# One decoder layer on one core: the stage behind the input projection ordered anew, a triple of weight slots between any two groups of small products, and page values and weights interleaved on SyncE

## The reference, cut to what matters

```python
h = rmsnorm(x) * (1 + scale1(c)) + shift1(c)
p = h @ w_in                       # 21 tiles of 128 columns here
#   NSA:   compressed blocks, top-16 selected blocks, window of 512, mixed by gates
#   mLSTM: 4 heads, chunkwise with running max; the samples one step from a state
#   pool:  trailing means over 2/4/8/16, a linear map per group
x = x + gate1(c) * (concat(nsa, mlstm, pool) @ w_out)
h = rmsnorm(x) * (1 + scale2(c)) + shift2(c)
x = x + gate2(c) * ((silu(a) * b) @ w_down)   # [a, b] = conv3(h @ w_up)
```

## Time and profile before

| | us |
|---|---|
| median of three runs | 843.7 (842.22 to 844.24) |
| the profiled execution | 844.35 |
| its span | 842.2 |
| TensorE busy, share of the span | 778.6 (92%) |
| VectorE | 516.3 (61%) |
| ScalarE | 329.5 (39%) |
| GpSimd | 308.1 (37%) |

### The profile page before, as it was taken

How to read it: one execution, slowest core, us unless ns; L and a number is a source line. 1 busy time by engine, 2 the same in 40 slices (tenths; PEclk the granted TensorE clock), 3 DMA queues, 4 the chain that set the end, 5 groups by cost and what they waited for, 6 DMA issues and landing times.

```text
span 842.2 us, 18847 instructions
## 1 busy us (share of the span) xinstructions
PE 778.6 (92%) x7517; PEld 717.9 (85%) x7517; DVE 516.3 (61%) x1026; ACT 329.5 (39%) x601; POOL 308.1 (37%) x163
## 2 busy tenths in 40 slices
PE   2899989999988898999989999999999999999994
PEld 2798979988866566669978999999999999999993
DVE  3745799994676799743765666665222676665324
ACT  4422322333241466643335554552213545544221
POOL 0042657572000344452422443444434434344440
PEclk9999999999698699998999999999999999999997
DMA  9964777786579544423721344342332432322312
GB/s 355 327 227 133 232 234 258 248 270 224 198 278 380 97 120 124 97 74 111 311 76 51 101 126 124 101 124 78 101 100 90 126 119 95 101 89 87 97 49 101
DMA packets 73141, 131.23 MB, mean 156 GB/s; under 512 B 12684, under 2 KB 47388, under 8 KB 72800
## 3 DMA queue, kind: packets, MB, share of 16 engines
q1 hardware_dynamic: 66928, 114.32, 42.3%
q10 hardware_dynamic: 6096, 15.73, 5.3%
q0 software_dynamic: 32, 0.00, 0.0%
HBM read 124.56 MB, written 9.12 MB: 159 GB/s over the span
## 4 chain that ended last, share of the span: by engine, by line
PE 77%; DVE 12%; issue 4%; DMA 3%; ACT 2%; SPq 1%; POOL 0%; DVEq 0%; ACTq 0%; POOLq 0%
PE ps L668 58%; PE ps L1016 2%; PE ps L1001 2%; PE ps L1038 2%; PE ps L1054 2%; PE ps L760 1%; DMA arena<-weights 1%; DMA raw<-weights 1%; DMA arena<-cache_keys 1%; DVE arena L2090 1%; PE ps L919 1%; PE ps L753 1%; DVE sq L1480 1%; PE ps L890 1%; DVE arena L1504 1%
## 5 line engine op out<-in xcount | busy, mean ns | idle before, releaser
L668 PE MATMUL ps<-hR,wR 128*128 128x260 f32 x3456 | 429.3, 286 | 7.8 <-ACT hR L1144 2.7
L668 PEld LDWEIGHTS ps<-hR,wR 128*128 128x128 f32 x3456 | 422.6, 191 | 12.4 <-issue 6.3
L631 POOL TENSOR_TENSOR wR<-raw,wR 128x1024 fp32r<-128x1024 f32 x92 | 225.4, 2450 | 298.7 <-ACT wR L1136 298.7
L1136 ACT ACTIVATE wR<-raw 128x1024 fp32r<-128x1024 f32 x94 | 99.5, 1058 | 214.6 <-PE ps L668 210.0
L668 PE MATMUL ps<-fR,wR 128*128 128x260 f32 x1056 | 128.1, 283 | 2.3 <-DVE fR L2061 2.0
L668 PEld LDWEIGHTS ps<-fR,wR 128*128 128x128 f32 x1056 | 127.0, 188 | 3.1 <-DVE fR L2061 2.4
L2085 DVE COPY arena<-arena 128x2 f32<-128x2 f32 x44 | 47.7, 1084 | 93.5 <-ACT arena L1427 93.5
L624 POOL TENSOR_SCALAR arena<-arena,fac 128x128 f32<-128x128 f32 (+3 forms) x32 | 40.3, 1263 | 133.0 <-DVE fac L1984 133.0
L612 POOL TENSOR_TENSOR arena<-arena,par 128x512 f32<-128x512 f32 x32 | 42.4, 1326 | 79.7 <-DMA arena<-cache_keys 75.1
L2046 DVE TENSOR_TENSOR t<-ps,mod 128x8 f32<-128x8 f32 x24 | 4.0, 167 | 108.7 <-PE ps L668 108.7
L1360 ACT ACTIVATE arena<-ps,nmx 128x128 f32<-128x128 f32 (+3 forms) x64 | 33.1, 524 | 19.8 <-DVE nmx L1975 19.7
(11 more groups left out here) (369 smaller groups left out, 845.3 us busy)
## 6 DMA issues: line engine op xcount, KB each, us to landing
raw<-weights SPq DMA_DIRECT2D x95, 512.0 KB, 3.7
arena<-cache_keys SPq DMA_DIRECT2D x128, 192.0 KB, 3.5
arena<-weights SPq DMA_DIRECT2D x27, 512.0 KB, 10.1
arena<-cache_values SPq DMA_DIRECT2D x128, 64.0 KB, 2.0
raw<-weights ACTq DMA_DIRECT2D x12, 512.0 KB, 8.5
arena<-weights ACTq DMA_DIRECT2D x9, 512.0 KB, 7.9
x<-xT SPq DMA_DIRECT2D x16, 260.0 KB, 4.0
out_y<-x SPq DMA_DIRECT2D x8, 260.0 KB, 2.2
```

The costliest lines, as they stand in the source:

```text
L631: nc.gpsimd.tensor_tensor(w_slot(i)[:, 1, :, :], raw[:, g % RAW, :, :], w_slot(i)[:, 0, :, :].bitcast(F32), ALU.subtract).then_inc(lo_read ...
L668: last = mm(ps[:, a + half, 0:TH], w_slot(i)[:, wp, k, :], src[:, hp, j, half * TH:(half + 1) * TH], start=(j == 0 and q == 0), stop=(j == ...
L1136: A(w_slot(i)[:, 0, :, :], raw[:, g % RAW, :, :], ACT.Identity).then_inc(hi_ready, 1)
```

## The change

On TensorE the helpers are called in another order; ScalarE's and VectorE's lists follow. `sample_rows` is cut into four helpers, and its products for the value rows go with those for the query and key rows (192 columns in one product instead of 128 and 64). The pool products use banks 4, 5 and 7 instead of 0, 1 and 6, and the turns of the mLSTM result banks 0 and 1; `side_mix` goes, and `scores(0)` waits for `mmix_ready`. ScalarE issues no weights in this stage any more; SyncE does, between the pages. `spread` is issued ahead of the window keys, and these in parts of six and two sequences. The window values go ahead of five outputs, and the first three slots of `w_out` behind the pages of sequences 2 and 3.

```diff
 # SyncE
-            sp.wait_ge(comp_done, 2 * NB)
-            sp.wait_ge(slc_scored, 2 * NB)
-            for b in range(0, NB, 4):
-                sp.dma_start(kwin[:, b:b + 4, :], winK[:, b:b + 4, :]).then_inc(win_landed, 16)
+            sp.wait_ge(rows_ready, 1)
+            sp.dma_start(spread, mro[0:4, :]).then_inc(side_landed, 16)
+            for half, first, last in ((2 * NB - 1, 0, 6), (2 * NB, 6, 8)):
+                sp.wait_ge(comp_done, half)
+                sp.wait_ge(slc_scored, half)
+                sp.dma_start(kwin[:, first:last, :], winK[:, first:last, :]).then_inc(win_landed, 16)
...
+            load_rows(2)
+            load_rows(3)
+            for g in range(N_A + RAW + EXTRA, N_A + 5 * RAW):
+                load_slot(g)
...
             sp.wait_ge(wsc_done, 2)
             load_values(0)
-            load_values(1)
+            for g in range(N_A + 5 * RAW, N_A + 7 * RAW):
+                load_slot(g)
+            load_value_half(1, 0)
+            for g in range(N_A + 7 * RAW, len(PART1)):
+                load_slot(g)
+            load_value_half(1, 1)
             sp.dma_start(cst[:, :], mC).then_inc(rec_landed, 16)
             sp.dma_start(o_fm, pT[:, T_KC:T_MK, 0:S]).then_inc(early_out, 16)
             sp.dma_start(o_vn, vn[:, :, :]).then_inc(early_out, 16)
+            sp.wait_ge(slot_done, len(PART1))
+            sp.wait_ge(mmix_ready, 1)
+            load_window(0)
+            load_window(1)
...
             load_values(2)
             load_values(3)
+            for g in range(len(PART1), len(PART1) + RAW):
+                load_slot(g)
 # TensorE: sample_rows cut up, the new order
+            def sample_heads(first):
+                for hh in range(first, first + 2):
+                    sel = every[:, 24 - 8 * hh:24 - 8 * hh + P]
+                    three = sn[0:NB, 0:768].rearrange("p (t h d) -> p t h d", t=3, h=4)[:, :, hh, :]
+                    mm(ps[:, 6, 0:192].rearrange("p (t d) -> p t d", t=3), sel, three, start=(hh == 0), stop=(hh == 3))
...
+            block_sums()
             triple(0)
             compressed_scores()
-            gate_columns()
+            triple(1)
+            sample_rows()
+            sample_heads(0)
             chunk_scores(0)
-            sample_rows()
-            block_sums()
+            window_scores(0)
+            sample_heads(2)
             chunk_scores(1)
+            sample_gates()
+            triple(2)
+            output_gates()
+            window_scores(1)
+            inside(0)
             triple_turn(0)
-            window_scores(0)
-            triple(1)
-            inside(0)
-            window_scores(1)
             chunk_scores(2)
+            inside(1)
+            triple(3)
+            chunk_scores(3)
             triple_turn(1)
             window_rows()
-            inside(1)
-            triple(2)
-            chunk_scores(3)
-            triple_turn(2)
-            triple(3)
             across(0)
             across(1)
+            triple(4)
+            triple_turn(2)
+            triple(5)
             triple_turn(3)
-            triple(4)
             inside(2)
+            triple(6)
             triple_turn(4)
             inside(3)
-            triple(5)
+            triple(7)
             across(2)
             across(3)
             triple_turn(5)
-            triple(6)
...
+            pooled_mix()
             triple_turn(6)
...
-            triple(7)
             triple_turn(7)
+            head_turns()
 # ScalarE
-                for n in range(N_A + 3 * g, N_A + 3 * g + 3):
-                    if n in BEFORE:
-                        load_weights(BEFORE.index(n))
 # VectorE, the new order
+            samples_cmp_weights()
+            samples_block_max()
             masked_rows(0)
             masked_rows(1)
             exponents(0)
-            samples_cmp_weights()
+            samples_block_sums()
+            samples_compare()
             prompt_cmp_scores()
+            samples_ranks()
+            samples_new()
             weighted(0)
-            samples_new()
-            samples_block_sums()
             weighted(1)
             masked_rows(2)
             masked_rows(3)
             exponents(1)
-            samples_block_max()
+            prompt_cmp_max()
+            weighted(2)
+            states(0)
             samples_selection()
-            states(0)
-            weighted(2)
-            samples_window_max()
             weighted(3)
             head_result(0)
             head_result(1)
-            states(1)
+            samples_window_max()
             samples_output_gates()
...
+            prompt_gates()
+            samples_weights(0)
+            prompt_cmp_weights()
+            states(1)
             head_result(2)
             head_result(3)
+            pooled_result()
+            samples_weights(1).then_inc(sp_ready, 1)
             dve.wait_ge(hT_done, 1)
-            V.tensor_tensor(mix[:, 4:6, 0:S], ps[:, 4:6, :], pT[:, T_MO:T_MO + 2, 0:S], ALU.mult).then_inc(mmix_ready, 1)
+            V.tensor_tensor(mix[:, 4:6, 0:S], ps[:, 0:2, :], pT[:, T_MO:T_MO + 2, 0:S], ALU.mult).then_inc(mmix_ready, 1)
```

More of the change, by code:

```diff
@@ L810, in _ @@
             last.then_inc(blocks_done, 1)
[L811 to L819, removed]
             def block_sums():
@@ L962, in _ @@
             triple_turn(5)
-            triple(6)
-            pe.wait_ge(pool_ready, 1)
-            pe.wait_ge(num_evac, 4)
-            for t in range(2):
-                mm(ps[:, t, :], par_("pw", t * P, (t + 1) * P), md[:, t, :], start=True, stop=True)
-                last = mm(ps[:, 6, t * NB:(t + 1) * NB], par_("pw", t * P, (t + 1) * P), mds[:, t, :], start=True, stop=True)
-            last.then_inc(pool_mm, 1)
-            triple_turn(6)
-            for t in range(2):
-                for i in range(ST):
-                    last = nc.tensor.transpose(ps[:, 4 + t, i * P:(i + 1) * P], hN[:, i, t * P:(t + 1) * P], ident)
-            last.then_inc(hT_done, 1)
-            triple(7)
+            pooled_mix()
+            triple_turn(6)
             triple_turn(7)
+            head_turns()
             def sample_flips():
@@ L1298, in window_read @@
                 A(sst[:, q * S:(q + 1) * S], ps[:, 7, :], ACT.Identity).then_inc(wsc_evac, 1)
-            def load_weights(g):
-                act.dma_start(raw_slot(g), wst[g, :, :].rearrange("p (k n) -> p k n", k=KD)).then_inc(landed(g), 16)
             def factors(t):
@@ L1677, in _, with samples_block_max @@
                     prompt_sums((h - 10) // 2, h % 2)
+            def samples_block_max():
+                for moved in sst_moved:
+                    dve.wait_ge(moved, 64 * NB // 2)
+                V.tensor_reduce(bmax[:, 0:32], sall[:, 0:NPG * P].rearrange("p (n k) -> p n k", k=64), AX, ALU.max)
             dve.wait_ge(blocks_done, NB)
@@ L1741, in samples_cmp_max @@
                 V.tensor_scalar(ssx[:, 1:2], ssx[:, 0:1], -SCALE, None, ALU.mult).then_inc(sx_in, 1)
-            def samples_block_max():
-                for moved in sst_moved:
-                    dve.wait_ge(moved, 64 * NB // 2)
-                V.tensor_reduce(bmax[:, 0:32], sall[:, 0:NPG * P].rearrange("p (n k) -> p n k", k=64), AX, ALU.max)
             def samples_output_gates():
@@ L1805, in prompt_cmp_scores, with prompt_cmp_max @@
                         last = V.tensor_tensor(p4, s4, madd, ALU.add)
-                link(last)
+                last.then_inc(pcx_ready, 1)
+            def prompt_cmp_max():
+                dve.wait_ge(pcx_ready, 1)
                 link(V.tensor_reduce(mx[:, 0, :], pc[:, :, 0:NCP], AX, ALU.max))
@@ L1891, in _ @@
-            V.tensor_tensor(pc[:, :, 0:NCP], pc[:, :, 0:NCP], mx[:, 3, :].unsqueeze(2).broadcast_to([P, 32, NCP]), ALU.mult)\
-                .then_inc(pc_ready, 1)
-            dve.wait_ge(hT_done, 1)
-            windows_moved(dve)
-            V.tensor_tensor(mix[:, 4:6, 0:S], ps[:, 4:6, :], pT[:, T_MO:T_MO + 2, 0:S], ALU.mult).then_inc(mmix_ready, 1)
-            dve.wait_ge(pool_mm, 1)
-            for t in range(2):
-                V.tensor_scalar(mix[:, 6 + t, 0:S], ps[:, t, :], par_("pool_s", t, t + 1), None, ALU.mult)
-                last = V.tensor_scalar(mix[:, 6 + t, S:T], ps[:, 6, t * NB:(t + 1) * NB], par_("pool_s", t, t + 1), None, ALU.mult)
```

142 lines of the change are left out of this document (84 added, 58 removed).

## The result

The changed kernel takes 839.09 us (median of 18 runs, 835.01 to 841.68), the kernel before, beside it, 844.77 us (18 runs, 841.23 to 847.56): ratio 0.9937 [0.992, 0.9955], so some 5.3 us faster. The forecast was 11 us.

The account below looks back on a forecast made before the run. TensorE, busy 92% of the span but partly at half clock, was taken as the bound. 844.35 less 11.5 (stage) plus 0.5 (attention) gave 833.35, the median 0.65 lower; stated 833.0, range 829 to 837, 8 in 10: 826.5 to 841.

Parts of the forecast that it names:

- the cause in the first half of the stage: TensorE from 218.4 to 231.8: thin products standing together, without idle time, brought the clock to 1.2 GHz.
- the walk to 231: TensorE's new order summed product by product from triple 0: `window_scores(1)` by 227.4, `inside(1)` to 232.5, triple 3 to 234.0.
- SyncE's wait for `spread`: Ahead of the broadcasts, 4.4 us: claimed to go, so broadcasts and slots 40 to 42 start up to 4.4 us earlier.
- rival 3: SyncE's queue: page issues above 0.656 us delay the slots, change slower; 848.8 us at 1.31 an issue, chance 0.13.
- rival 2: The stage: clock doesn't follow the order, both low stretches remain (11.8 us); 843.5 us, no change, chance 0.09.
- a new wait of 3.3 us: TensorE at triple 5: slots 52 to 54 come behind 16 page issues, so it ends at 245.0, not 241.7.
- slots 58 to 60 land by 252.0: Stage's last slots, issued behind eight more pages (5.2 us), land by 252.0, so triple 7 ends at 252.5.
- The 3.7: Slot loads in the stage: a slot lands 3.7 us behind its issue, the next two at 1.3 us each.
- rival 1: The stage: one low stretch remains or a new one comes, likely behind triple 5's wait; 5.1 to 6.7 us, 839, chance 0.17.
- gives back 0.5: Attention at `sample_values(2)`: window values late behind SyncE's outputs and slots, wait between 0 and 5.7 us, taken as 0.5.
- Rival 4: Attention's opening: the third low stretch goes too, 4.5 us less, 828.5 us, chance 0.16.

Follow-up runs that it names:

- in a row: Changed kernel with its thin products next to each other ahead of the dense ones: 843.94 us, ratio 0.9978 to the kernel before.
- orders alone: New orders of TensorE, ScalarE and VectorE, with the transfers of the kernel before the change: 840.5 us, ratio 0.9911.
- slots first: Changed kernel with slots 52 to 60 issued ahead of all 32 pages of sequences 0 and 1: 845.28 us, ratio 0.9995.
- relay: Changed kernel with all stage slots first, then sequence 0's pages, small outputs, window values, sequence 1's pages, and later transfers as in late list alone: 840.06 us, 0.996.
- finer interleave: Changed kernel with eight pages, slots 52 to 54, eight pages, slots 55 to 60, then sixteen pages: 835.9 us, ratio 0.9886.
- late list alone: Changed kernel, SyncE's list behind the stage altered: small outputs earlier, sequence 2's window values and first `w_out` slots ahead of sequence 3's pages: 834.19 us, 0.9887.
- transfers alone: New transfers under the old orders of TensorE, VectorE and ScalarE: 848.95 us, ratio 1.003 to the kernel before.
- triple 1 moved: Changed kernel with triple 1 moved behind `sample_gates`, next to triple 2: 841.56 us, ratio 0.9964.
- relay with the finer interleave: As the relay, with eight pages ahead of slots 52 to 54 and eight behind them: 842.89 us, ratio 0.9982.
- both repairs: Changed kernel with finer interleave, late list, and from sequence 4 on each window right behind its own pages: 831.98 us, ratio 0.9839.

## Why the prediction was wrong

**What held.** The direction, the cause in the first half of the stage, and the walk to 231: measured from the stage's first product, `inside(0)` starts at 19.75 us (forecast 19.7) and triple 3 at 25.15 (24.8). The first low stretch came with thin products together, and the order removed it (13.4 us before, 16.6 under the old orders, 10.3 in a row again, none in orders alone). `sample_heads` took 0.91 for two heads (taken 1.5 for four, measured 1.8). SyncE's wait for `spread` is gone (broadcasts at 204.16), and TensorE's entry moved by 0.56 only, within what it varies by anyway. SyncE's 16 pages took 8.87 us (taken 10.5), so rival 3, the dear page issue, fell; rival 2 fell with the first stretch. VectorE waits for TensorE to the end (for `across`, until 256.62, for 3.95 us).

**The step that failed: "a new wait of 3.3 us" at triple 5, with a clock that stays up behind it, and "slots 58 to 60 land by 252.0".** The total of the wait was right, 3.2 us, but not its place. TensorE came to triple 5 later by 1.6 us (1.3 of it in triple 3 at 1.2 GHz), waited there for ScalarE for 0.64, which I had at nothing, and for a slot for 0.41; then 0.83 at triple 6 and 0.54 and 1.40 at triple 7. I had let the third slot of a group land 6.3 us behind the group's issue (3.7 from the earlier trace rows and twice 1.3). Slots 52 to 54 did (237.04 to 243.36); 55 to 57 took 8.9 (239.65 to 248.50); 58 to 60 were issued only at 247.22, behind eight pages that started later than I had them, and took 7.5. The 3.7 was the median of one of the two sets of places, over the whole kernel. The page of before had dearer ones right beside it, for the other set of places, which takes triples 5 and 7, and for what ScalarE issued (KB each, median us to landing):

```profile
arena<-weights SPq DMA_DIRECT2D x27, 512.0 KB, 10.1
raw<-weights ACTq DMA_DIRECT2D x12, 512.0 KB, 8.5
```

In after the nine loads of slots 52 to 60 landed 3.7 to 7.9 us behind their own issue, with a median of 4.9.

So triple 7 ended 3.3 us behind the forecast. Then the clock fell at 255.5, just behind those waits: `across`, turn and pool products ran at 1.2 GHz for 6.9 us, of which half, 3.4, is an estimate of the loss, and head turns ended 6.3 us behind the forecast, `scores(0)` 5.4 (VectorE's tail was 0.9 shorter than taken). This is rival 1 in its mechanism, "a new one comes, most likely behind the 3.3 us wait", and its 839 is the measured time; I had given it 0.17. That the two agree so closely is partly luck: in the profile the stage was 5.4 us dearer than forecast and the attention 1.1 cheaper, and the median then lay 1.9 above the profiled execution, where I had it 0.65 below. The dependence on the waits is shown by the kernels that have TensorE's order of after from triple 4 on. Where the waits for slots came to 0.60, 0.88 and 1.05 us in all (slots first, relay, finer interleave), the clock held from triple 4 to the attention's opening; in the eight with 1.58 to 3.59 us it fell for some 3 to 10 us. How much wait it takes is not settled: orders alone had 0.95 us there and fell. The Trainium skill, TensorE: Matmul & The Clock Gate, section HAM oscillation, puts falls down to TensorE's waiting for transfers between groups. The fall at 255.5 agrees with it in kind (four waits of 0.41 to 1.40 us ahead), those at 218.6 above and at 231.6 do not (no idle time). I used the disagreement in the first stretch to discount the rule in the second, where it held.

**The term that was too small: attention "gives back 0.5".** In the profile it was right (0.85 of wait, attention 0.6 shorter than before). Over the runs it was more, by an estimate some 4: the late list alone brings 0.5%. How much after loses there in its median no profile shows. The cause, as far as these profiles tell, is the one named, SyncE's outputs and slots ahead of the windows, but I took the lower end because the outputs find DMA engines that are idle. What binds there is SyncE itself: 20.6 us of issue for 32 pages, which start only when the stage has ended and the outputs are issued and landed, 6.5 us behind `scores(0)` in after but 9.7 to 11.2 in the three profiles that wait 4.0 to 6.8 us.

**Rival 4** didn't come: the third stretch is as long as before. Two slips in the sums moved little: 4.0 us from 253.6 lead to 257.6 and not 257.1, and by my own figures the head turns end 2.4 us ahead of `scores(0)` and not 1.6 (measured idle: 1.46).

The Trainium skill, DMA: Bandwidth & Descriptors, section Issuing engines are not separate DMA queues, holds the issue time to be usually small beside the transfer. Not here: 64 KB pages take 0.55 to 0.66 us each of SyncE's time (the bytes of one, at the 398 GB/s of the earlier trace rows, an estimated 0.16), and the order of SyncE's list alone moved this kernel between 0.984 and 1.000.

## What to carry to other kernels

Where the clock falls though TensorE never idles, look for products of few rows or columns in a row and put dense ones between them; then count again every wait for a transfer behind, because a few waits of a microsecond or less can be followed by half clock for seven. When a stage becomes shorter, follow the queue that feeds the next stage past the stage's end: small transfers issued in a row (16 pages 8.9 us, 32 pages 20.6) decide what comes late, and each large one that is needed soon must go ahead of them, without pushing all of them behind the stage.

## What the runs showed of the hardware

- TensorE fell to 1.2 GHz with no idle time in the 8 us ahead in seven kernels (218.4 before, 231.6 after, 218.6 in a row, 215.9 transfers alone, 219.3 finer interleave, 221.9 triple 1 moved, 221.4 relay with the finer interleave), amid or right behind products of few rows or columns. It stayed low for 10.3 to 16.6 us where these stood in a row, and for 3 to 4 us where they stood apart.
- What decides the short falls isn't settled (each kernel has one profile): under one and the same TensorE order the clock fell at 231.6 in after, at 219.3 and 229.5 with the finer interleave alone, at 221.4 and 231.6 in the relay with the finer interleave, and nowhere before 241 with slots first, the relay, the late list alone or both repairs.
- A 512 KB load landed at a median of 3.6 us on one set of slots and 8.9 on the other in the same kernel (after); the first set is filled all through the kernel, the second is where the loads of triples 5 and 7 go, amid pages.
- Behind four waits for transfers of 0.41 to 1.40 us TensorE ran at 1.2 GHz for 6.9 us (after, 255.5).
- With spare dense products ahead of a sparse opening the low stretch there was 3.6 us and not 13.7, in one profiled execution, at no measurable gain in the median.
